# A two-block network in one launch: the first tile's queries from fp32 products, its output product in tile 1, gate sums in other places, and a second stage that starts on constants already there

## What is computed

```python
mod = silu(c) @ ada_w[0] + ada_b[0]              # 1024 -> 3 x 1024
shift, scale, gate = split(mod)
h = rmsnorm(x, norm_g) * (1 + scale) + shift
q, k, v, low_rank, r = split(h @ w_in)           # 512, 512, 1024, 16, 1024
log_decay = log_sigmoid(low_rank @ w_alpha + b_alpha) / 16
o = gated_linear_attention(q, k, v, log_decay)   # 4 heads, chunks of 64, a running state
x1 = rmsnorm(x + gate * ((rmsnorm(o) * silu(r)) @ w_out), final_g)
mod2 = silu(c_2) @ w_mod_2 + b_mod_2             # second block: the same, with its own mixers
h2 = rmsnorm(x1, g_pre_2) * (1 + scale2) + shift2
out = x1 + gate2 * rmsnorm(mixers(h2) @ w_out_2, g_post_2)
```

## Time and profile before

| | |
|---|---|
| median of 3 runs | 2235.39 us (2235.12 to 2235.45) |
| the profiled execution | 2235.16 us, its span 2233.3 us |
| PE busy | 2078.4 us (93%), 19816 products |
| PEld busy | 1447.7 us (65%) |
| DVE, ACT, POOL busy | 1480.4, 1176.8, 622.2 us (66%, 53%, 28%) |
| mean DMA | 78 GB/s, 174.57 MB |

### The profile page before, as it was taken

The page is one execution under the profiler, slowest core; times in us unless marked ns, Lnnn a source line. Parts: engine busy times, 40 slices in busy tenths (PEclk is TensorE's granted clock), DMA queues, the critical chain, the costliest instruction groups (busy, mean ns, idle before and its releaser), DMA issues. The chain is left out here.

```text
span 2233.3 us, 48522 instructions
## 1 busy us (share of the span) xinstructions
PE 2078.4 (93%) x19816; PEld 1447.7 (65%) x19816; DVE 1480.4 (66%) x2616; ACT 1176.8 (53%) x2561; POOL 622.2 (28%) x590
## 2 busy tenths in 40 slices
PE   4889999999999999499999999999997899999997
PEld 4536666666666666289889998889996344444342
DVE  7655555555555554247766777776776888888886
ACT  3734444444434444234544554544554888878885
POOL 3700001000000000145343334343333344444442
PEclk9989999999999999799999999999999899999999
DMA  8652222222222231810000110010103922110110
GB/s 312 189 165 87 86 78 93 78 78 83 78 91 88 85 97 40 257 36 28 28 32 28 38 40 28 28 31 28 39 30 83 272 67 66 40 57 39 39 38 29
DMA packets 139806, 174.57 MB, mean 78 GB/s; under 512 B 48576, under 2 KB 99904, under 8 KB 139584
## 3 DMA queue, kind: packets, MB, share of 16 engines
q1 hardware_dynamic: 139296, 170.41, 24.1%
q10 hardware_dynamic: 288, 1.05, 0.1%
HBM read 122.39 MB, written 49.03 MB: 77 GB/s over the span
## 5 line engine op out<-in xcount | busy, mean ns | idle before, releaser
L343 POOL TENSOR_TENSOR g_stage<-g_stage,g_nh_row 128x1024 f32<-128x1024 f32 x16 | 52.3, 3271 | 752.5 <-DVE g_stage L731 752.5
L2101 POOL TENSOR_TENSOR s_hi<-s_sp,b_cols 128x512 bf16<-128x512 f32 x144 | 163.0, 1132 | 285.2 <-DVE s_sp L2210 283.9
L1663 PE MATMUL m_bank<-h_hi,w_all 128*128 128x128 bf16 (+1 forms) x1280 | 218.5, 220 | 23.3 <-POOL m_arena L1240 19.7
L1663 PE MATMUL m_bank<-m_h_hi,w_all 128*128 128x128 bf16 (+1 forms) x1280 | 217.1, 219 | 4.0 <-DVE m_arena L1576 2.1
L1664 PE MATMUL m_bank<-h_lo,w_all 128*128 128x128 bf16 (+1 forms) x1280 | 218.2, 220 | 0.0
L1665 PE MATMUL m_bank<-h_hi,w_all 128*128 128x128 bf16 (+1 forms) x1280 | 218.1, 220 | 0.0
L1665 PE MATMUL m_bank<-m_h_hi,w_all 128*128 128x128 bf16 (+1 forms) x1280 | 216.8, 219 | 0.0
L1664 PE MATMUL m_bank<-m_h_lo,w_all 128*128 128x128 bf16 (+1 forms) x1280 | 216.8, 219 | 0.0
L824 PE MATMUL g_bank<-w_all,h_hi 128*128 128x512 bf16 x512 | 197.5, 386 | 13.9 <-ACT g_stage L462 7.7
L825 PE MATMUL g_bank<-w_all,h_hi 128*128 128x512 bf16 x512 | 197.1, 385 | 0.0
L826 PE MATMUL g_bank<-w_all,h_lo 128*128 128x512 bf16 x512 | 196.6, 384 | 0.0
(11 more groups left out here) (394 smaller groups left out, 6026.1 us busy)
## 6 DMA issues: line engine op xcount, KB each, us to landing
g_piece<-in_w_dram SPq DMA_DIRECT2D x64, 268.0 KB, 3.3
g_piece<-in_w_mod_t_dram SPq DMA_DIRECT2D x48, 256.0 KB, 3.1
w_hi<-g_piece_hi SPq DMA_DIRECT2D x64, 134.0 KB, 1.9
w_lo<-g_piece_lo SPq DMA_DIRECT2D x64, 134.0 KB, 2.1
g_xs<-in_x_dram SPq DMA_DIRECT2D x16, 512.0 KB, 3.9
g_stage<-in_ada_w_dram SPq DMA_DIRECT2D x16, 512.0 KB, 8.3
s_xr<-x SPq DMA_DIRECT2D x16, 512.0 KB, 4.1
out_dram<-s_xr SPq DMA_DIRECT2D x16, 512.0 KB, 2.6
```

Of the source, the lines that this page charges most:

```text
L343: pool.tensor_tensor(r_sb.rearrange("p (h e) -> p h e", h=GH), r_sb.rearrange("p (h e) -> p h e", h=GH), nh_row[:].unsqueeze(1).broadcast_ ...
L1663: pe.matmul(out, l_hi, r_hi, start=(k == 0), stop=False)
L2101: pool.tensor_tensor(hi[g % NH][:], sp_[k], one_col.broadcast_to([P, 512]), ALU.mult).then_inc(s["hi_done"], 1)
```

## The change

1. **Modulation in pieces.** The shift part is 8 pieces of 128x1024, of which DVE sums 7 and PE multiplies the eighth by c itself; the scale part is 16 half-wide pieces. PE's sums, `modulation` and `h_make` go in two halves.
2. **Tile 0's queries.** `first_queries` multiplies the fp32 query weights by the fp32 h. Their high and low parts, needed from tile 1 on, are made later: three highs on ACT between gate and keys, the lows at the end of tile 0. Tile 0's x norm is on ACT, and the h of tile 1 is made on ACT.
3. **Twelve places.** The ring has 12 places; the four new ones are in the accumulator of the modulation.
4. **Tile 0's output product** goes into banks KV0 and KV1 in tile 1, behind `turn_x(2)`; `y_add_first` reads x from a second load. In tile 1 the products for the next state stand last.
5. **Gate sums** go in seven groups from the end of tile 0 to behind `x_norm(2)`, through two places of their own, loaded in between the w_out pieces.
6. **Side pieces** lie in tiles 2 to 14: 8 in tiles 2 to 6, 9 in tiles 7 to 14. c_2 is loaded and its silu made in tile 2.
7. **Stage 2's constants.** `MixInputs` holds identity, columns and small vectors, made or loaded in stage 1. The last x1 tile is written from its own buffer, and nobody waits for its store until tile 14 of stage 2. PE's first product waits for no constant; ACT and DVE wait for four memsets; the window's bias is made inside tile 0.

The core of the diff (`SHIFTS` is KB - 1, so 7, and `SCALES` is 2 * KB, so 16):

```diff
+            for kb in range(SHIFTS):
+                dve.wait_ge(slot_in[kb], 16)
+                weighted_sum(acc[:, 0:D], arena[:, kb * D:(kb + 1) * D], kb, kb)
+            for n in range(SCALES):
+                kb, half = n % KB, n // KB
+                dve.wait_ge(scale_in[n], 16)
+                weighted_sum(acc[:, D + half * 512:D + (half + 1) * 512], scale_piece(n), kb, SHIFTS + n)
+            modulation(0)
+            h_make(0, halves=(0,))
+            modulation(1)
+            h_make(0, halves=(1,))
...
+            def first_queries():
+                for h in range(GH):
+                    for kb in range(KB):
+                        if h == 0:
+                            pe.wait_ge(q_in[kb], 16)
+                        ins = pe.matmul(G0[:, h * T:(h + 1) * T], q_cols[kb][:, h * GDK:(h + 1) * GDK], xn[:, kb * T:(kb + 1) * T],
+                                        start=(kb == 0), stop=(kb == KB - 1))
+                ins.then_inc(s["q_done"], 1)
...
-                if not first:
-                    y_products(i - 1)
-                if i == 1:
-                    sum_gate()
-                wait("y_used", 2 * i - 1)
+                if i == 1:
+                    pe.wait_ge(s["og_lo_done"], 2)
+                elif i > 1:
+                    y_products(i - 1)
+                    pe.wait_ge(s["y_used"], 2 * i - 1)
...
                 turn_x(i + 1)
+                if i == 1:
+                    pe.wait_ge(s["state_done"], 1)
+                    sum_gate()
+                    y_products(0)
+                    pe.wait_ge(s["gate_ready"], 2)
+                elif not last:
+                    keys_values(i)
...
+                if i == 1:
+                    pe.wait_ge(s["y_used"], 2)
+                    keys_values(i)
...
-            sp.wait_ge(s["x1_out"], 16 * NT)
+            sp.wait_ge(mix.small_in, 16 * len(mix.small))
+            sp.wait_ge(s["x1_out"], 16 * (NT - 1))
...
+                        if i == 2:
+                            c2_silu()
+                        piece_highs(side(i)[2:5])
...
-            pe.wait_ge(s["consts_ready"], 1)
```

SP's loads of gate pieces (half, kb) and w_out pieces r now stand so: (0,0), (0,1), (0,2), (1,0); r 0 to 7; x of tile 2; the two rows; (0,3) to (0,6); r 8 to 11; (0,7), (1,1); r 12 to 15; (1,2) to (1,7). A gate piece waits until the one two before it in its pair of places has been summed:

```diff
+                    t = gate_no(half, kb)
+                    if t >= 2:
+                        wait("gate_done", t - 2 + 2 + (t - 2) // (KB - 1))
+                    sp.dma_start(gate_slot[t % 2], src).then_inc(gate_slot_in[t % 2], 16)
```

More of the change, by code:

```diff
@@ L254, in _ @@
+            load_gate(0, 4)
+            load_gate(0, 5)
+            load_gate(0, 6)
+            for r in range(KB, KB + 4):
+                load_wo(r)
+            load_gate(0, 7)
+            load_gate(1, 1)
+            for r in range(KB + 4, 2 * KB):
+                load_wo(r)
+            for kb in range(2, KB):
+                load_gate(1, kb)
+            wait("gate_done", 2 * KB)
+            sp.dma_start(x_first, x[0, 0:T, :]).then_inc(s["x0_in"], 16)
             sp.dma_start(b2_col, b_mod_2).then_inc(s["b2_in"], 16)
@@ L288, in store @@
                 sp.dma_start(x1[(i - 1) * T:i * T, :], xo).then_inc(s["x1_out"], 16)
-            sp.wait_ge(s["gate_done"], 2 * KB)
+            wait("w_lo_p", ALL_P + 2 * KB)
             load_piece(0)
             load_piece(1)
-            for i in range(1, NT - 1):
-                behind = 0 if i == 1 else 3
-                for j in side(i)[:behind]:
+            wait("x2_done", 2)
+            sp.dma_start(c2_row, c_2_row.partition_broadcast(P)).then_inc(s["c2_in"], 16)
+            store(1)
+            for i in range(2, NT - 1):
+                for j in side(i)[:3]:
                     piece_away(j)
                 load_x(i + 1)
-                for j in side(i)[behind:]:
+                for j in side(i)[3:]:
                     piece_away(j)
@@ L301, in _ @@
             load_x(NT)
+            for dst, src in mix.small:
+                sp.dma_start(dst, src).then_inc(mix.small_in, 16)
             for n in range(2):
@@ L688, in tile @@
                 if i == 1:
-                    gate_sums(1)
-                    gate_whole()
-                if i == 1:
-                    y_add(i - 1, 1 - par, range(0))
-                    pieces(side(i)[:5])
-                else:
+                    gate_sums(7, 10)
+                if i > 1:
                     pieces(side(i)[:2])
-                    if not first:
-                        y_add(i - 1, 1 - par, side(i)[2:3])
+                    y_add(i - 1, 1 - par, side(i)[2:3])
                     pieces(side(i)[3:5])
@@ L963, in tile @@
                 turn_x(i + 1)
-                if not last:
-                    pe.wait_ge(s["klT_copied"], i + 1)
-                    wait("state_done", i)
-                    for h in range(GH):
-                        ins = pe.matmul(KV[h // 2][:, (h % 2) * GDV:(h % 2 + 1) * GDV], klT[:, h * GDK:(h + 1) * GDK],
-                                        v_sb[:, h * GDV:(h + 1) * GDV], start=True, stop=True)
-                    ins.then_inc(s["kv_done"], 1)
+                if i == 1:
+                    pe.wait_ge(s["state_done"], 1)
+                    sum_gate()
+                    y_products(0)
+                    pe.wait_ge(s["gate_ready"], 2)
+                elif not last:
+                    keys_values(i)
                 wait("state_done", i)
@@ L1304, in tile @@
                 pool.tensor_tensor(av_hl[:, 1, slot, :], av, av_hl[:, 0, slot, :], ALU.subtract).then_inc(s["av_lo"], 1)
-                if not first:
+                if first:
+                    window_bias()
+                else:
                     split_ya(i - 1)
```

540 lines of the change are left out of this document (341 added, 199 removed).

## The result

The changed kernel takes 2199.97 us (median of 4 runs, 2198.89 to 2202.38), the kernel before 2235.42 beside it: ratio 0.9843, 95% interval 0.9826 to 0.986, so 35.5 us less. I had given 2193 with 2186 to 2202. The direction and the range hold; the gain is 6.5 us smaller than the forecast's 41.9. The profiled execution took 2198.89 us, its span 2196.8.

What follows compares the result with a forecast made beforehand. TensorE, busy 2078.4 of 2233.3 us, was taken as the bound, its idle time as the gain. From 2235.2: -2.1 - 26.3 - 1.3 + 1.0 - 13.2 = -41.9, given as 2193 us, range 2186 to 2202.

Steps and rivals of the forecast that it cites:

- The start: Before tile 0's keys: h whole at 33.5, fp32 queries end near 43.4, keys start 2.4 us sooner.
- Tile 0: Tile 0 together with the start: tile 1 begins 2.1 us sooner, bounds -7 and +4.
- my three signs of being wrong: Tile 1 over 62 us; tile 1 starting after 91; a new bias or sqk wait in stage 2's first tile.
- I take 1.2 each for the four: End of tile 0: four query lows on DVE beside POOL's cost 1.2 us each, 4.8 us.
- locked: Tile 0: shared DVE-POOL port, or slow-clock queries, gains nothing or loses up to 4 us; 2197 us; chance 0.16, both causes.
- Tile 1: Idle time and slow clock go as gate sums and y products move: 57.0 us, -26.3, bounds -28 and -16.
- I leave 1.6 us for idle time: Tile 1: 1.6 us of PE idleness remains, for the low-rank product's copy and a key copy.
- tight place: Tile 1: the last gate piece's sum ends at 36 us into the tile, PE wants it at 37.
- late gate: Tile 1: last gate piece misses the x turns by one or two loads, 5 to 10 us; 2201 us; chance 0.10.
- Tile 2 and the ninth piece: Tile 2 loses its slow start, -1.3 us; a ninth side piece in eight tiles costs +1 us, 0 to +6.
- the slower rival: Stage 1: ninth side piece misses its slot in eight tiles, 6.7 us each, 54 in all; 2247 us; chance 0.03.
- The boundary: Between stages: no wait for the last x1 store or POOL's constants, -13.2 us, bounds -5.6 and -14.7.

Runs made afterwards that it cites:

- t0_lows_alone: Changed kernel, but POOL leaves out its four odd query-weight lows and ACT copies the weights to their places instead: 2198.10 us.
- t0_highs_late: Changed kernel, but ACT makes the first four w_out highs behind the high part of tile 1's h: median 2200.56 us, ratio 0.9836.
- Ten pieces: Changed kernel, but side pieces are 8 in tiles 2 to 10 and 10 in tiles 11 to 14: 2209.96 us.
- t1_exps_first: Changed kernel, but in tile 1 ACT makes the exponentials ahead of w_out highs 8 to 11: median 2200.35 us, ratio 0.9829.

## Why the prediction was right, and where it was wrong

**The start: right.** I had the sums end at 28.8, h whole at 33.5 and the queries end at 43.4. DVE's sums ended at 29.07, h at 33.16; 64 passes took 9.19 us from 33.21 on (forecast 9.9), and the queries ended at 42.4. Keys began at 44.2 (forecast 45.8), and values at 53.6 (55.0): up to here the change was 1.4 us better than forecast.

**Tile 0: wrong, +1.05 instead of -2.1.** Of my three signs of being wrong this is the one that came: tile 1 starts after 91, at 92.0. The step that failed is "I take 1.2 each for the four". The lows take 1.58 beside each other, and not only the four at the end: of DVE's 16 lows of w_in from 45 us on ten show 1.4 to 1.65, and the six that fell where POOL made none 0.7. The four query lows took 6.3 us instead of the 4.8, and POOL, which began its four 1.05 later, ended 7.3 us after DVE had begun: 2.5 us more than I had. From the start of the values to tile 1 I had 33.9 us and it took 38.4. The other 2.0 us of that difference stay open, since the prediction does not work out its chain from 55.0 to 88.9 step by step. The queue that I had named (the w_out highs wait for the query lows, and the copy of r and h stand behind them) is what happened; `t0_lows_alone` shows the price and `t0_highs_late` the queue. I had taken 1.2 between rows of 0.69 and 1.6, although the row at 1.6 was the one with POOL running, as it does here. The rival "locked" described this best; it priced the tile at nothing gained to 4 us lost. The fp32 queries I had priced at -2.4 at the keys; with their late lows counted in they bring 2.5 at tile 1's start, and making the lows cheap or moving the highs out of their way brings about 3 more. That the ring's four places are worth 3 to 4 us there was in no step of mine.

**Tile 1: right in the main, size off by 2.5 us.** 57.0 was forecast, 59.5 measured. I took away the whole 28 us of idle time and slow clock, and named the gate sums and the y products for it. The sums are shown to carry about half. Of the rest I had not seen that 6.5 us were PE's waits for ACT behind w_out highs, and 4.2 ended behind side pieces: both went with other parts of the change, so the sum was right there without knowing why. "I leave 1.6 us for idle time" was the term: it is 4.0 us, so 2.4 more. Another 1.6 are products at the low clock behind the stall for h_lo (55.5 busy, less tile 3's 52.0 and 1.95 for the ones products; the granted clock is 0.81 from 92 to 100 us and 1.00 after), and those ones products took 1.95 and not 3.1, since they now run at the high clock. I had seen that w_out 8 to 11 stand behind gate pieces in SP's queue, and looked only at the y products, "due 40 us in". I had not followed them into ACT's queue, where their highs stand ahead of the exponentials 15 us in. The gate itself, my "tight place", was late by 1.3 us: the rival "late gate" is right in its place and priced too high (5 to 10). That the chain of gate sums also fixes the end of the tile, so that a better start is lost where the sums do not move with it (`t0_highs_late`) and kept where they do (`t0_lows_alone`), became visible only when single waits were taken away.

**Tile 2 and the ninth piece: right.** -0.5 us against -0.3. Ten pieces show how near the edge it stood: the slower rival's mechanism exists, and begins one piece later.

**The boundary: right,** 13.4 against 13.2, in both its terms: 5.4 for the store (5.6) and 6.6 for the constants (7.7 less 1.3). PE stood 6.7 us ahead of stage 2, against the 6.5 forecast. DVE and POOL met no new wait in the first tile; POOL's bias ended at 951.0, and sqk's split waited 0.85 us for ACT after it, so of the 3 us that I had left free 0.85 remained.

The range held because the bounds of tile 0 (-7 to +4) and tile 1 (-28 to -16) had been carried into it; the own range of the likeliest case, 2190 to 2196, did not. The time lies in the band of the rival "late gate" (2198 to 2203), but not by its mechanism: the gate cost 1.3 us.

## What to carry to other kernels

When work is moved off the path into the queues of other engines, follow each moved instruction into every in-order queue that it enters, and ask what stands behind it there: here a load behind a gate piece on SP became a late exponential on ACT and then a wait of PE. Price an operation by a row taken with the same neighbours running. A wait that is taken away pays only when what stands behind it moves too: `t0_highs_late` and `t1_exps_first` each gave nothing that the times can tell from the change. `all_a`, with four gate places, the exponentials first and half of the query lows where both engines had stood idle, gave 7 us. And when an experiment gives back half of a gain, look in the trace of before for what the other half waited for, before giving it to the second idea.

## What the runs showed that I had not expected

- A 128x512 subtraction takes 0.62 us on DVE alone and 1.58 beside a like one on POOL, whose own goes from 1.16 to 1.57. Two engines together make a pair in 1.58 us, against 1.78 one after the other and, by the same rows, about 1.24 for two on DVE alone: in this case moving a low from DVE to POOL costs time while both are busy.
- Of the 23.8 us that tile 1 became shorter, 17.1 were idle time and 6.7 busy time: the waits had cost more than another third of their length in products at the low clock (1.2 of it in the gate's ones products, 3.10 us at a clock of 0.62 before and 1.95 at 1.00 now). The clock can also take back what an edit wins: in `t1_exps_first` 2.0 us less idle time came with 2.0 us more busy time.
- The same code of stage 2 took 1280.9 to 1283.4 us in different runs, more than some of the edits are worth.
